# Layer 0's attention: five page groups and the token stores issued in the pooling stage, the ring moved, one or two phases to a step

## The reference

```python
def fox_attention(q, k, v, logf, pos0):            # 8 heads of 64
    cum = jnp.cumsum(logf.astype(jnp.float32), axis=1).transpose(0, 2, 1)
    ...
        logits = jnp.einsum('bqhd,bkhd->bhqk', qi, k, preferred_element_type=jnp.float32) * scale
        logits = logits + ci[..., :, None] - cum[:, :, None, :]
        mask = (k_pos[None, :] <= q_pos[:, None])[None, None]
        p = masked_softmax(logits, mask)
        return jnp.einsum('bhqk,bkhd->bqhd', p.astype(v.dtype), v)
...
    k_all = jnp.concatenate([k_past, k], axis=1)   # samples: k_past = pool[page_table]
    v_all = jnp.concatenate([v_past, v], axis=1)
    o_fox = fox_attention(q, k_all, v_all, lf_all, pos0).reshape(B, T, FOX_WIDTH)
    o_pool = pool_mixer(u_ext, pos0, pool_map, pool_scale)
    y = jnp.concatenate([o_fox, o_pool], axis=-1) @ w_out
```

## Time and profile before

| | us |
|---|---|
| median of 3 runs | 2381.47 (2381.38 to 2385.14) |
| the profiled execution | 2380.61 |
| its span | 2378.9 |
| mean granted PE clock | 0.916 of full speed |
| PE busy | 2075.4 (87% of the span) |
| DVE busy | 1359.4 (57%) |
| ACT busy | 787.3 (33%) |
| POOL busy | 274.6 (12%) |

### The profile page before, as it was taken

How to read it: one execution, slowest core, us unless ns; L and a number is a source line. 1 busy time by engine, 2 the same in 40 slices (tenths; PEclk the granted TensorE clock), 3 DMA queues, 4 the chain that set the end, 5 groups by cost and what they waited for, 6 DMA issues and landing times. The chain is left out here.

```text
span 2378.9 us, 47747 instructions
## 1 busy us (share of the span) xinstructions
PE 2075.4 (87%) x18117; PEld 1874.5 (79%) x18117; DVE 1359.4 (57%) x2556; ACT 787.3 (33%) x1407; POOL 274.6 (12%) x436
## 2 busy tenths in 40 slices
PE   5986898779999896997779987988987786999998
PEld 3963675559999896994579977988974486999998
DVE  5425431358887644336366657877753357888732
ACT  3111331115544202012256654444431215544300
POOL 0002533100000000000022222212223100000000
PEclk8987897889999998997789998999998997999999
DMA  9335989652333321225320004334449613333221
GB/s 373 93 108 221 337 280 374 226 206 69 107 105 84 113 74 38 73 72 228 128 93 2 2 17 138 107 107 128 115 158 326 235 63 81 97 107 101 93 85 63
DMA packets 238296, 322.58 MB, mean 136 GB/s; under 512 B 18424, under 2 KB 195013, under 8 KB 230764
## 3 DMA queue, kind: packets, MB, share of 16 engines
q1 hardware_dynamic: 215893, 240.23, 30.9%
q0 software_dynamic: 21728, 79.19, 9.6%
q10 hardware_dynamic: 447, 0.11, 0.0%
HBM read 311.56 MB, written 16.42 MB: 138 GB/s over the span
## 5 line engine op out<-in xcount | busy, mean ns | idle before, releaser
L2604 PE MATMUL ps<-CHi,W1H 128*128 128x256 f32 x768 | 222.2, 289 | 37.1 <-DVE CLo L2707 37.1
L2605 PE MATMUL ps<-CLo,W1H 128*128 128x256 f32 x768 | 220.1, 287 | 0.0
L2606 PE MATMUL ps<-CHi,W1L 128*128 128x256 f32 x768 | 219.9, 286 | 0.0
L942 PE MATMUL ps<-XHup,WLup 128*128 128x272 f32 x640 | 185.1, 289 | 0.0
L942 PE MATMUL ps<-XHup,WHup 128*128 128x272 f32 x640 | 183.8, 287 | 1.3 <-DVE G L1091 1.3
L942 PE MATMUL ps<-XLup,WHup 128*128 128x272 f32 x640 | 184.5, 288 | 0.0
L2604 PEld LDWEIGHTS ps<-CHi,W1H 128*128 128x128 f32 x768 | 150.3, 196 | 39.1 <-DVE CLo L2707 28.3
L483 PE MATMUL ps<-XHdn,WHdn 128*128 128x272 f32 x704 | 148.4, 293 | 12.4 <-DMA PT<-in_cache_fox_v 5.4
L2125 DVE TENSOR_REDUCE NM<-ps 128x1 f32<-128x128 f32 (+1 forms) x224 | 89.6, 403 | 119.3 <-PE ps L2004 82.8
L2605 PEld LDWEIGHTS ps<-CLo,W1H 128*128 128x128 f32 x768 | 150.5, 196 | 0.0
L2606 PEld LDWEIGHTS ps<-CHi,W1L 128*128 128x128 f32 x768 | 150.3, 196 | 0.0
(11 more groups left out here) (564 smaller groups left out, 5354.5 us busy)
## 6 DMA issues: line engine op xcount, KB each, us to landing
H<-in_w_up SPq DMA_DIRECT2D x72, 512.0 KB, 5.0
Wearly<-in_w_mod SPq DMA_DIRECT2D x24, 1024.0 KB, 12.7
RAWdn<-in_w_down SPq DMA_DIRECT2D x14, 1408.0 KB, 7.2
RAWin<-in_nsa_w_in SPq DMA_DIRECT2D x20, 512.0 KB, 3.7
RINGf<-in_cache_fox_k SPq DMA_DIRECT2D x34, 256.0 KB, 5.1
Wmod<-in_w_mod SPq DMA_DIRECT2D x8, 1024.0 KB, 18.1
RAWfirst<-in_ab_w_in SPq DMA_DIRECT2D x16, 512.0 KB, 3.8
Wlate<-in_w_mod SPq DMA_DIRECT2D x8, 1024.0 KB, 8.2
```

What stands on the lines that cost most here:

```text
L942: last = self.nc.tensor.matmul(self.ps[:, bank + b, 0:HALF], wt[:, w, k, :], x[:, k, :], start=start and k == 0 and n == 0, stop=k == 3 an ...
L2604: nc.tensor.matmul(out, WH[:, sig, k, w], hi, start=(k == 0 and m == 0), stop=False, skip_group_check=True)
L2605: nc.tensor.matmul(out, WH[:, sig, k, w], lo, start=False, stop=False, skip_group_check=True)
L2606: last = nc.tensor.matmul(out, WL[:, sig, k, w], hi, start=False, stop=(k == KU - 1), skip_group_check=True)
```

## The change

The ring's first five slots become one tile RINGf, placed by `beyond` at a fixed distance (RINGS) so that it lies where Wearly's slots lie; QBA, the values VE and two tiles of probabilities move into PT's upper half instead. `PastAttention` is made before `pooling`. In `pooling`, SP issues the token stores after the last w_mod load, without waiting for them, and the even pages of groups 0 to 4 after the pool states; ACT issues the odd ones. Group k waits until 20 + k bites are done. PE's transposes of the pool states move from ahead of bite 13 to ahead of bite 17, with their wait for the two loads. In `fox_prompt`, SP starts with group 5, which still waits for `stored` and `valued`; POOL issues groups 5 and 6 after the first two heads' queries. ACT copies the values before the first head's keys, DVE places the queries before the first subtraction, POOL takes a head's queries 6 steps ahead of their use instead of 12. After each step the engines run two phases, after each third step one.

```diff
@@ pooling, SP @@
                     for q in range(meal[1] + meal[0]["slots"], 3 * KD):
                         self.mod_load(sp, meal[0], q)
+                    store(sp)
                     sp.dma_start(o["pool_s"][0, :, 0:EX - TS, :], i["state_pool"][0, :, TS:EX, :]).then_inc(st, 16)
...
+                    for k in range(past.FIRST):
+                        past.ahead(sp, 0, k, meal[0]["used"])
                     sp.wait_ge(st, 16 * (2 + NB))
@@ pooling, PE @@
-                    pe.wait_ge(ld, 32)
-                    for g in range(4):
-                        last = nc.tensor.transpose(ps[:, 0, g * P:g * P + NB * EX], SR[:, g * P:(g + 1) * P], self.ident[0:NB * EX, 0:NB * EX])
-                    last.then_inc(tr, 1)
                     for q in range(meal[1], 3 * KD):
+                        if q == 2 * KD + 1:
+                            pe.wait_ge(ld, 32)
+                            for g in range(4):
+                                last = nc.tensor.transpose(ps[:, 0, g * P:g * P + NB * EX], SR[:, g * P:(g + 1) * P], self.ident[0:NB * EX, 0:NB * EX])
+                            last.then_inc(tr, 1)
@@ pooling, ACT @@
-                    for n in (1, 2):
-                        self.mod_rows(act, meal[0], n)
+                    self.mod_rows(act, meal[0], 1)
+                    for k in range(past.FIRST):
+                        if k == past.FIRST - 2:
+                            self.mod_rows(act, meal[0], 2)
+                        past.ahead(act, 1, k, meal[0]["used"])
@@ PastAttention @@
-        self.ring = sb("RINGf", [P, 3, self.QUARTERS, 512])
-        self.low = PT[:, 8:16, :].rearrange("p c n -> p (c n)")[:, 0:2 * self.QUARTERS * 512].rearrange("p (s a f) -> p s a f", s=2, a=self.QUARTERS)
-        self.QBA = sb("QBA", [P, NB, 4 * R])
+        self.ring = kernel.beyond("RINGf", [P, self.FIRST, self.QUARTERS, 512], RINGS)
...
+        low = PT[:, 8:16, :].rearrange("p c n -> p (c n)")
+        self.QBA = low[:, 0:1024].rearrange("p (b r) -> p b r", b=NB)
+        self.VE = low[:, 1024:3104].rearrange("p (j h x) -> p j h x", j=PT_TILES, h=FH)
+        self.PR, self.PTT = low[:, 3104:3616], low[:, 3616:4128]
...
+    def phases(self, step):
+        return 1 if step % 3 == 2 else 2
...
         elif k >= self.FIRST:
-            for signal, value in self.rows_free:
-                engine.wait_ge(signal, value)
+            engine.wait_ge(self.stored, 64)
+            engine.wait_ge(self.valued, 1)
...
+    def ahead(self, engine, parity, k, bites):
+        engine.wait_ge(bites, 20 + k)
+        self.load(engine, parity, k)
...
-        for k in range(self.FIRST):
-            for parity in range(2 if k < self.BY_SP else 1):
-                self.load(sp, parity, k)
-        store(sp)
         for k in range(self.FIRST, len(self.groups)):
             self.load(sp, 0, k)
@@ PastAttention, POOL @@
-        for k in range(self.BY_SP, self.FIRST):
-            self.load(pool, 1, k)
-        yield
         for k in range(self.FIRST, self.SLOTS):
             self.load(pool, 1, k)
         yield
@@ PastAttention, DVE: the eight copies into QBA and the signal `queries` move ahead of the first yield @@
@@ prompt_attention @@
-            query_at.setdefault(max(0, first_use["q", h] - 12, last_use["q", h - 4] + 1 if h >= 4 else 0), []).append(h)
+            query_at.setdefault(max(0, first_use["q", h] - (6 if beside else 12), last_use["q", h - 4] + 1 if h >= 4 else 0), []).append(h)
...
-                        if values_act and k == keys_made[2]:
+                        if values_act and k == keys_made[0]:
                             values_act(act)
...
-                    if beside:
+                    for _ in range(beside.phases(step) if beside else 0):
                         next(phases, None)
```

More of the change, by code:

```diff
@@ L57 @@
 EARLY = 112416
+RINGS = 49824
 LATE = 63616
@@ L1474, in _, with store_tokens @@
                     copy(dve, 1)
-    def store_tokens(self, sp, TOK, stores, st):
+    def store_tokens(self, sp, TOK, stores, st, wait=True):
         o, count = self.o, 0
@@ L1487, in store_tokens, with pooling @@
             count += 1 + (NB if row else 1)
-        sp.wait_ge(st, 16 * count)
-    def pooling(self, PT, meal, NC, bias):
+        if wait:
+            sp.wait_ge(st, 16 * count)
+    def pooling(self, PT, meal, NC, bias, past, store):
         nc, ps, i, o, H = self.nc, self.ps, self.i, self.o, self.H
@@ L1610, in __init__, with tiles @@
         self.PER = self.PAGES // self.QUARTERS
-        self.ring = sb("RINGf", [P, 3, self.QUARTERS, 512])
-        self.low = PT[:, 8:16, :].rearrange("p c n -> p (c n)")[:, 0:2 * self.QUARTERS * 512].rearrange("p (s a f) -> p s a f", s=2, a=self.QUARTERS)
-        self.QBA = sb("QBA", [P, NB, 4 * R])
-        self.PR, self.PN = sb("PR", [P, 512]), sb("PN", [R, NS])
+        self.ring = kernel.beyond("RINGf", [P, self.FIRST, self.QUARTERS, 512], RINGS)
+        self.sp_full, self.pool_full = ([sem(f"fd_{n}_full{s}") for s in range(self.SLOTS)] for n in ("sp", "pool"))
+        self.used = sem("fd_used")
+        self.groups = [("k", 0, n) for n in range(self.PER)]
+        for b in range(NB):
+            self.groups += [("k", b + 1, n) for n in range(self.PER) if b + 1 < NB] + [("v", b, n) for n in range(self.PER)]
+        self.index = {g: k for k, g in enumerate(self.groups)}
+    def tiles(self, sb, sem, valued):
+        R, PT = self.R, self.PT
+        self.valued = valued
+        low = PT[:, 8:16, :].rearrange("p c n -> p (c n)")
+        self.QBA = low[:, 0:1024].rearrange("p (b r) -> p b r", b=NB)
+        self.VE = low[:, 1024:3104].rearrange("p (j h x) -> p j h x", j=PT_TILES, h=FH)
+        self.PR, self.PTT = low[:, 3104:3616], low[:, 3616:4128]
+        self.PN = sb("PN", [R, NS])
         self.SN, self.NM, self.RS = sb("SN", [R, NS]), sb("NMf", [P, 3]), sb("RS", [P, 2])
-        self.PTT, self.PTN = sb("PTT", [P, 512]), sb("PTN", [NS, R])
+        self.PTN = sb("PTN", [NS, R])
         self.LEAST, self.ROW, self.W = sb("LEAST", [1, R]), sb("ROW", [1, P]), sb("W", [P, 3])
@@ L1620, in __init__ @@
         self.const_in = sem("fd_const")
-        self.sp_full, self.pool_full = ([sem(f"fd_{n}_full{s}") for s in range(self.SLOTS)] for n in ("sp", "pool"))
-        self.used, self.queries, self.scores, self.maxima, self.probs = (sem("fd_" + n) for n in ("used", "queries", "scores", "maxima", "probs"))
+        self.queries, self.scores, self.maxima, self.probs = (sem("fd_" + n) for n in ("queries", "scores", "maxima", "probs"))
         self.turned, self.turned_out, self.new_turned, self.new_out, self.pv, self.o_out, self.o_turned, self.heads_out = (sem("fd_" + n) for n in (
@@ L1626, in __init__ @@
             "m_turned", "row_ready", "row_exp", "spread", "weighed", "summed", "share_read", "dc"))
-        self.groups = [("k", 0, n) for n in range(self.PER)]
-        for b in range(NB):
-            self.groups += [("k", b + 1, n) for n in range(self.PER) if b + 1 < NB] + [("v", b, n) for n in range(self.PER)]
-        self.index = {g: k for k, g in enumerate(self.groups)}
+    def phases(self, step):
+        return 1 if step % 3 == 2 else 2
     def slot(self, k):
         s = k % self.SLOTS
-        return self.ring[:, s, :, :] if s < 3 else self.low[:, s - 3, :, :] if s < 5 else self.rows[:, s - 5, :, :]
+        return self.ring[:, s, :, :] if s < self.FIRST else self.rows[:, s - self.FIRST, :, :]
     def load(self, engine, parity, k):
@@ L2158, in _ @@
                     for h in query_at.get(step, ()):
-                        if beside and h == 2:
-                            next(phases)
                         own, other, src = heads[h]["own"], heads[h]["other"], heads[h]["src"]
@@ L2187, in _, with fox_prompt @@
                     pass
-    def fox_prompt(self, PT, TOK, NC, EP, bias, first, store, stored):
+    def fox_prompt(self, PT, TOK, past, bias):
         nc, H = self.nc, self.H
@@ L2193, in fox_prompt @@
             T, sems = self.prompt_tiles(sb, sem, FH * PT_TILES, [TP] * 3, (ID, MASK))
-            past = PastAttention(self, sb, sem, PT, TOK, NC, EP, first, stored, sems["values_act"])
-            VE = sb("VE", [P, PT_TILES, FH, HD + 1])
+            past.tiles(sb, sem, sems["values_act"])
+            VE = past.VE
             def ones(dve, link):
@@ L2210, in fox_prompt @@
                                    value=lambda j, h=h: VE[:, j, h, :]))
-            self.prompt_attention(T, sems, groups, heads, keysets, [H[:, c, 0:TP] for c in range(4)], ones, lambda sp: past.sp(sp, store), past, values)
+            self.prompt_attention(T, sems, groups, heads, keysets, [H[:, c, 0:TP] for c in range(4)], ones, past.sp, past, values)
     def gather(self, pool, table, col, where, dst, loaded):
@@ L2248, in fox_mixer @@
                 self.to_tokens(PT, 4, 8, TOK, 6)
-                self.pooling(PT, (self.early, 13), NC, bias)
-                self.fox_prompt(PT, TOK, NC, EP, bias, first,
```

(5 more changed lines are left out.)

25 lines of the change are left out of this document (12 added, 13 removed).

## The result

The changed kernel takes 0.9933 of the time of the kernel before, 95% interval 0.9917 to 0.9950: 12 to 20 us less, about 16. The medians of seven runs each are 2367.18 (2365.93 to 2374.65) and 2385.1 us (2381.38 to 2390.55). The forecast was 32 us less, in a range whose upper end (2364) the median lies beyond. The direction was right, the forecast size was twice what came.

The account below looks back on a forecast made before the run. DMA engines idle during the prompt's heads and are the limit afterwards. Attention stage 6.4 + 135.9 + 43.3 = 185.6 us against 216.0, with 2.0 from pooling 32.4 us off: 2349 us, range 2339 to 2364.

Parts of the forecast that it names:

- the pages after step 37: Steps 38 to the end: 12 groups still to load and 6.4 us after make 39.3 us, under PE's 43.3.
- The boundary: End of the pooling stage: bites start 3.9 us earlier, moved loads and stores cost little; 2.0 us gained.
- rival D: Stage boundary: it waits for page loads in flight, until about 238 us; 4.6 us back, 2354 us, chance 0.05.
- Steps 0 to 37: the waits: Steps 0 to 37: 2.4 us of page wait and 3.0 of copied-probability waits go; 135.9 us in all.
- rival A: Paired phases: PE waits up to 1.5 us for the exponential row, a sample costs 17.05; 2362 us, chance 0.19.
- my lower price: Steps 0 to 37: a sample's PE work at full clock beside prompt work, 12.6 us; 13.8 was taken.
- The start: Start of the attention stage: first unit at 5.5 us, first page product at 6.4 instead of 9.0; 2.6 us gained.
- the 2.74 us a group: Page loads in the attention stage: one group of 1.049 MB at 383 GB/s takes 2.74 us.
- PE's work in the tail: Steps 38 to the end: the 32 phases left take PE 43.3 us, against 98.3 before.
- C, the lockstep: Two-phase steps: each ends in a 1.5 us wait of PE for ACT or DVE; 2407 us, chance 0.03.

Follow-up runs that it names:

- e9: The changed kernel, but from group 7 on only the first 256 of the 512 numbers in each page row are loaded; ratio to before 0.9870.
- e3: The changed kernel, but SP issues four of its ten page loads after the constants, at the start of the attention stage; ratio to before 0.9921.
- e6: As e3, and the token stores are issued after the pool states instead of before them; ratio to before 0.9916.
- e5: The changed kernel, but from group 7 on only the upper 64 token rows of each page are loaded; ratio to before 0.9908.

## Why the prediction was wrong

**The step that failed: the pages after step 37.** "The pages allow it: 19 groups left, 7 of them already in the ring". There were not 7. When the last unit's values ended, at 387.4 us, PE had used 44 groups (not 45: the phases of step 37 come after its values), so 20 were left. 47.75 had landed, so only 3.75 lay ready. From 387.4 to 431.5 us the DMA engines brought 44.1 x 382 = 16.8 MB, less 0.5 for the output weights: 15.6 groups' worth still to come (part of the rest was on its way), where I had 12. I had checked supply by an average over steps 0 to 37, 110 us of loads in 136, and taken the spare for a full ring at its end. A ring of seven can't save what is not fetched in a hole. It was last full, with 28 groups used and the 7 next landed or under way, in the hole before 346.6 us; by 387.4 12.8 more had landed, and PE had taken 16, since most of the last steps carry little of the prompt: 7 + 12.8 - 16 = 3.8. With these figures my own sum for the pages reads 15.6 x 2.74 = 42.7 us instead of 32.9, and 9.4 from the end of the DMA's work to the stage's end instead of 6.4: 52.1 instead of 39.3, over PE's 43.3 and near the 53.5 measured. (That is a reading back, since the 15.6 come from the same 44.1 us; the count from the full ring gives 16.2 groups still to land without them.) e9 shows PE's own share of it as 42.9, where the forecast had 43.3: the work was sized right, the limit was not. 10.2 us of the shortfall.

**The boundary.** "SP's ten page loads have moved too, and are at most 1.5 us of issue after the last bite", and the token stores' move was costed as hidden. Only the last pair waits for the last bite, but SP came to its first page load only at 226.86, after it had stood 8.3 us at the last token store, and then needed 11.06 us. The gain in the bites was as large as its upper bound (4.1 us, bound 3.9), the stage gained -0.3. This is about rival D's size (4.6) by another cause, and e3 and e6 took it apart. I had counted the moved issues on the queue, but not where the queue stood when it came to them. 2.3 us.

The Trainium skill's rule, page "DMA: Bandwidth & Descriptors", section "Queues, rings and completion order", that the engines take queues in turn, would have cost the weights up to 4.1 us behind ACT's six loads. First the rows: the weights were issued 4.8 us earlier in the stage (206.45 - 204.32 = 2.1 against 208.13 - 201.20 = 6.9), and the last bite came 4.1 earlier, so ACT's loads, issued from 213.5 us while weights were still coming, cost some 0.7, or 1.4 if one counts from the last weight load (issued 5.5 us earlier). The two queues did share the engines. The DMA queues from 222 to 228 us (q1 is SP's, q10 ACT's; packets, MB, share):

```profile
q1 hardware_dynamic: 617, 1.23, 53.9%
q10 hardware_dynamic: 615, 1.13, 49.2%
```

The two move alike, though three of SP's four token stores (2.2 MB) had been issued before ACT's first load. There the trace agrees with the rule and not with the order of issue. Before the last weights landed, from 213.5 to 224.4 us, ACT's queue had moved 0.75 MB, half of its 1.57.

**Steps 0 to 37: the waits.** 141.2 against 135.9. The forecast took off half of the 6.1 us of waits for copied probabilities "since ACT and DVE get more time per step". They rose to 8.2, and rival A's waits appeared beside units: 2.8 us for the row, 1.7 for the probabilities. That is 13.2 us of waits, where I had 3.1. The samples themselves were cheaper than my lower price. Steps 0 to 37 without waits and at full clock, as an estimate: (141.2 - 13.2) x 0.91 = 116.5 after; before, (108.7 - 8.7) x 0.90 = 90.0 (8.7 is 6.3 and the 2.4 for a page). So 26 phases cost 26.5 us, 11.2 a sample, against 12.6 to 17.05. Against the forecast the waits are 9.9 us more and the rest 4.6 less: 5.3 us short. Of rival A the waits for copies and the lack of a gain in the pooling stage came as it said, and its row waits came beside units, but at 2.8 us where it had put 7.7 on the samples. The 10.2 us of the tail stand in no rival; that A's 2362 lies near the measured time is partly luck.

**The start** was 0.9 us late: the first unit began 6.3 us into the stage instead of 5.5. The eight copies into QBA took 3.23 us instead of 1.50, with POOL at work on PT in the same microseconds:

```profile
240.22 3.23 DVE L1893 COPY PT<-PT 64x32 f32<-64x32 f32 x8
```

They now write into PT, too. Which of the two doubles them was not tried. The four parts, 10.2, 2.3, 5.3 and 0.9, are the 18.7 us between the 32.4 us forecast and the 13.7 of the two profiled stages.

**What held.** The direction; that the early loads remove PE's 4.27 us wait; the 2.74 us a group; that the pages do not limit steps 0 to 37 (e9); PE's work in the tail. C, the lockstep, did not come: PE waits 13.2 us in 26 pairs, 0.5 a pair, where C had 1.5 and broke even at 0.83.

## What to carry to other kernels

Supply and demand of a ring can't be compared by averages over a stretch: find the last moment at which the ring was full, and count bytes and use from there to the end. When instructions are moved past a barrier onto a queue, add up that queue's whole timeline up to the barrier, issues at which it stands still (8.3 us here) and the waits at its end among it. What two halves of a change are worth alone need not add up to what they are worth together (4, 5.5 and 14 to 16 us of the whole time here), so price the pair, and once it is in, shift the mix until both resources end at once (2 to 2.33 phases a step here, not 1.67). And before a stage is compared between two profiles, compare its granted clock: e3 and e6, with the same waits up to step 37, lie 9 us apart (197.6 and 206.3) at clocks of 0.95 and 0.88.

## What the runs showed of the hardware

- Loading 64 of 128 partitions (e5) halved the bytes but hardly the engines' time: after step 37 168 GB/s at a share of 0.85, against 382 GB/s at 1.03 in the changed kernel. Halving each row to 1 KB over all 128 partitions (e9) brought 189 GB/s at 0.65, so it did relieve them.
- SP stood 8.3 us at one small store (the last of the four token stores, in the rows of SP above) with 7.4 MB of its own loads and stores issued before it in 6 us; the same store took 7.3 us in e6. What held it is not shown; that its queue was full is a guess.
- Two queues with work, SP's and ACT's, moved 1.23 and 1.13 MB from 222 to 228 us in the changed kernel, in 617 and 615 packets, although 2.2 MB of SP's token stores had been issued before ACT's first load.
- The same kernel, with the same waits, had a granted clock of 0.91 and 0.89 over steps 0 to 37 in two profiles, and kernels with the same waits there 0.88 to 0.95. That is 7 to 17 us of a stretch of 140, and nothing in these runs says why.
